# A fused two-block transformer kernel: scan operations in another order, squares of the norms added on GpSimd, rotary halves swapped by DMA

## The chip, the cores and the metric

The kernel runs on one core of a Trainium2 chip. A core has TensorE (PE in the profile; PEld is its weight load), VectorE (DVE), ScalarE (ACT), GpSimd (POOL) and the sync engine (SP), each with its own instruction stream; they wait for one another through semaphores. All numbers are float32. The metric is the time of one execution on the device in microseconds (us); lower is better.

## The reference, cut to what matters

256 tokens go through a first block (attention in three branches, a gated feed-forward part with a short convolution), and then, beside 256 context tokens, through two layers of a second block. The width is 1024. What the change touches:

```python
def rmsnorm(x, g, eps=1e-6):
    xf = x.astype(jnp.float32)
    y = xf * lax.rsqrt(jnp.mean(xf * xf, axis=-1, keepdims=True) + eps)
    return (y * g.astype(jnp.float32)).astype(x.dtype)

def apply_rope(x, cos, sin):            # on q and k of the latent tokens
    ...
    return jnp.concatenate([x1 * c - x2 * s, x1 * s + x2 * c], axis=-1).astype(x.dtype)

def ssd_chunked(x, dt, a, bm, cm, h0, need_y):   # once forward, once backward
    ...
    cb = jnp.einsum('bclgn,bcsgn->bclsg', cc, bc)
    y = (jnp.einsum('bclsg,bclsgr,bcsgrp->bclgrp', cb, lmat, xc)
         + jnp.einsum('bclgn,bcgrpn,bclgr->bclgrp', cc, h_in, jnp.exp(cs)))

def ssd_output(yf, yb, xs, z, ssd_d, ssd_norm_g, w_ssd_o):
    y = (yf + yb + ssd_d[:, None] * xs).reshape(b, n, SSD_D_INNER)
    return rmsnorm(y * jax.nn.silu(z), ssd_norm_g) @ w_ssd_o

def merge(att, ssd, ga, gs):
    return (jax.nn.sigmoid(ga) * (att @ w_attn_o) + jax.nn.sigmoid(gs) * ssd) @ w_out
```

`x` of the scan is the output of a convolution over 5 tokens (its taps) and a silu.

## The kernel before

Activations lie in SBUF with the features on the 128 partitions: `X` is the residual stream, `H` the normed input, 8 tiles of 512 columns (columns 0 to 255 are the latent tokens, 256 to 511 the context). All weights come as one stream of 1 MB chunks (128 x 8 x 256) through a ring of four buffers, loaded by SP as soon as TensorE is done with the chunk four before. A chunk of 16 matmuls writes two PSUM banks of a pair in `PB`; two pairs take turns, and TensorE waits on `evacuated` until VectorE and ScalarE have read a pair. The order on every engine is written out by hand, and each step waits for counts of semaphores. Layer 0 of the second block works on T = 512 columns (latent and context), layer 1 mostly on 256. `pe_fast` is a variant of a projection with seven products for eight, for which GpSimd first makes four sums of each weight chunk (`pool_sums`, L498 to L503, two chunks ahead), and VectorE puts the results together (`dve_fast`).

**Norms.** The squares of a norm's 8 tiles are written to SBUF, and `norm_sums` (L582) has TensorE add them over partitions and tiles: 8 matmuls with a matrix of 1/1024. ScalarE takes the root (`norm_root`, L589), VectorE the reciprocal (L595), then multiplies each tile (L2060), ScalarE adds the shift (L1499). For n2, n4, m21 and final (`sums_behind`) the matmuls of tiles 0 and 1 follow the second group of the projection before, those of 2 and 3 the third, those of 4 to 7 the last. m10c is the norm of the context columns, behind the first group of `down`. For m20 and m11 (512 columns) all eight stand at the end: VectorE adds the last result to `X` (L2376), ScalarE squares it (L599), TensorE sums.

**Rotary part.** While TensorE computes the four chunks of v (L1043), it also multiplies each of the 16 tiles of q and k by a matrix `rot` that swaps halves of 32 rows with a sign (L1066), one after each fourth of a chunk. VectorE multiplies the result by sin (L2100), GpSimd the tile by cos (L2485), VectorE adds (L2105). A barrier of all engines follows.

**Scan.** `scan_group` runs for 8 groups. Per group TensorE transposes (L1177), makes chunk states (L1198), applies them (L1212) and computes the products inside a chunk (`within`, L1229; 4 a group in layer 0, 2 in layer 1), and between these it projects the next group (L1146) and z (L1127). VectorE updates states and reads their results (`states`, L2233 to L2250), adds the skip product D*x (L2253), multiplies the decays with the scores (`masked`, L2265), applies the taps of the next group (`taps`, L2202; this frees the banks), and adds the inner products to Y (`sum_y`, L2272). At the end stand four chunks of gates gs (`project_gs`, L1160), the sum of squares of the normed output (L1282), its root (L1723) and the sigmoids of the gates (L1728).

The loop in VectorE's order:

```python
for g in range(SSD_GROUPS):
    states(g)
    per = 4 // len(units)
    for u in range(len(units)):
        masked(g, u)
        taps(g + 1, range(per * u, per * u + per))
    sum_y(g)
```

## Time and profile before

| | us |
|---|---|
| median of 3 runs | 3190.84 (3190.33 to 3196.2) |
| the profiled execution | 3196.1 |
| its span, first to last instruction | 3194.3 |
| TensorE busy | 3053.8 (96%) |
| VectorE busy | 1194.8 (37%) |
| ScalarE busy | 779.6 (24%) |
| GpSimd busy | 522.9 (16%) |
| mean granted TensorE clock | 0.987 |

Times in the rows are from the span's start. A row of a timeline is a group of equal instructions: start, length to the end of the last, engine, line, operation, output and inputs, count, and in square brackets the idle time of the engine ahead of it and what ended it. A float matmul has two records, so x16 are eight matmuls. The length of a row of matmuls includes the drain of the last; the difference of two starts does not. The granted clock is 1.00 for 2.4 GHz; its lower level is 1.2 GHz.

### The profile page before, as it was taken

Reading aid. Unit: us, or ns where it says so; the run is one execution under the profiler, and the core shown is the slowest. Engines: PE = TensorE matmul, PEld = TensorE weight load, DVE = VectorE, ACT = ScalarE, POOL = GpSimd, SP = SyncE. Lnnn points to the kernel's source line nnn. Section 1 sums busy time; section 2 is a strip of 40 time slices with the busy share of each in tenths; the row PEclk is TensorE's granted clock in tenths of the full one; section 3 lists DMA queues with packets and bytes.
Section 4 is the critical chain, followed back from the end, with each engine's and each line's share of the span. In section 5 each row is a group of like instructions: output and inputs, shape, how many; then the busy total and the mean of one; then the engine's idle time right before and its main releaser. Section 6 shows DMA issues by size and latency. Waiting matters only on the chain.

```text
span 3194.3 us, 35650 instructions
## 1 busy us (share of the span) xinstructions
PE 3053.8 (96%) x13958; PEld 2288.5 (72%) x13958; DVE 1194.8 (37%) x2286; ACT 779.6 (24%) x1697; POOL 522.9 (16%) x544
## 2 busy tenths in 40 slices
PE   8989899999999999999999999999999999989998
PEld 6766788887865545555548688887876766678887
DVE  1244232213236645555533542333146555531100
ACT  1012121201013324555520120111013355530000
POOL 0000110002210101121234233442210011110100
PEclk9999999999999999999999999999999999999999
DMA  6455334442235222222212122222211332224342
GB/s 232 155 210 203 119 120 156 149 143 90 93 115 215 93 94 92 106 93 98 88 60 86 66 93 79 93 87 85 93 66 53 120 106 93 105 97 153 132 158 93
DMA packets 60830, 365.66 MB, mean 114 GB/s; under 512 B 5818, under 2 KB 17146, under 8 KB 18320
## 3 DMA queue, kind: packets, MB, share of 16 engines
q1 hardware_dynamic: 48768, 334.67, 29.2%
q10 hardware_dynamic: 10944, 25.36, 2.3%
q0 software_dynamic: 976, 3.63, 0.3%
q8 instruction: 101, 1.65, 0.2%
q14 instruction: 41, 0.34, 0.0%
HBM read 362.37 MB, written 1.28 MB: 114 GB/s over the span
## 4 chain that ended last, share of the span: by engine, by line
PE 88%; DVE 8%; ACT 2%; issue 2%; DMA 0%; POOL 0%; POOLq 0%; DVEq 0%; ACTq 0%
PE PB L348 11%; PE PB L1146 10%; PE PB L465 9%; PE PB L392 9%; PE PB L974 7%; PE PA L465 6%; PE PB L1127 6%; PE PB L867 6%; PE PS L465 5%; PE PB L1043 3%; PE PB L1160 3%; DVE work L2202 2%; PE PA L1229 1%; PE PA L1198 1%; PE PA L1212 1%
## 5 line engine op out<-in xcount | busy, mean ns | idle before, releaser
L1146 PE MATMUL PB<-H,ring 128*128 128x512 f32 (+1 forms) x1024 | 428.1, 566 | 0.0
L1146 PEld LDWEIGHTS PB<-H,ring 128*128 128x128 f32 x1024 | 191.8, 190 | 184.6 <-issue 179.1
L392 PE MATMUL PB<-work,ring 128*128 128x256 f32 x1280 | 277.6, 379 | 0.0
L392 PEld LDWEIGHTS PB<-work,ring 128*128 128x128 f32 x1280 | 243.2, 190 | 33.1
L348 PE MATMUL PB<-H,ring 128*128 128x256 f32 x960 | 213.0, 385 | 10.4 <-ACT H L1499 7.5
L974 PE MATMUL PB<-H,ring 128*128 128x256 f32 x992 | 214.3, 379 | 0.0
L348 PEld LDWEIGHTS PB<-H,ring 128*128 128x128 f32 x960 | 185.4, 193 | 38.0 <-issue 12.0
L974 PEld LDWEIGHTS PB<-H,ring 128*128 128x128 f32 x992 | 188.5, 190 | 25.6
L1127 PE MATMUL PB<-H,ring 128*128 128x512 f32 (+1 forms) x512 | 182.0, 508 | 14.9 <-DVE work L2202 14.9
L2202 DVE SCALAR_TENSOR_TENSOR work<-PB,par,work 128x510 f32<-128x510 f32 (+3 forms) x256 | 181.0, 713 | 12.6 <-ACT work L1594 5.8
L867 PE MATMUL PB<-H,ring 128*128 128x256 f32 (+1 forms) x640 | 179.7, 436 | 1.5 <-ACT mod L1387 0.9
L348 PE MATMUL PB<-work,ring 128*128 128x256 f32 (+1 forms) x544 | 155.8, 446 | 7.1 <-POOL work L2446 2.4
L867 PEld LDWEIGHTS PB<-H,ring 128*128 128x128 f32 x640 | 122.6, 197 | 49.5 <-issue 35.3
L1127 PEld LDWEIGHTS PB<-H,ring 128*128 128x128 f32 x512 | 98.9, 199 | 78.5 <-issue 70.5
L465 PE MATMUL PB<-work,sums 128*128 128x256 f32 x680 | 150.8, 379 | 0.0
L2519 POOL TENSOR_TENSOR work<-work 128x256 f32<-128x256 f32 x96 | 59.7, 643 | 542.6 <-ACT work L1616 440.6
L498 POOL TENSOR_TENSOR sums<-ring 128x512 f32<-128x512 f32 x53 | 69.0, 1301 | 469.7 <-PE PA L465 224.3
L348 PEld LDWEIGHTS PB<-work,ring 128*128 128x128 f32 x544 | 104.1, 192 | 56.5 <-issue 37.8
L465 PEld LDWEIGHTS PB<-work,sums 128*128 128x128 f32 x680 | 129.2, 190 | 17.6
L1655 ACT ACTIVATE work<-sums,work 128x128 f32<-128x128 f32 x384 | 117.1, 389 | 81.8 <-PE PA L1229 81.4
L465 PE MATMUL PA<-work,sums 128*128 128x256 f32 x528 | 118.5, 379 | 0.0
L1043 PE MATMUL PB<-ring,H 128*128 128x256 f32 x512 | 115.7, 379 | 0.0
(326 smaller groups left out, 4344.6 us busy)
## 6 DMA issues: line engine op xcount, KB each, us to landing
ring<-stream SPq DMA_DIRECT2D x315, 1024.0 KB, 4.8
sums<-cs_rows ACTq DMA_DIRECT2D x16, 1024.0 KB, 4.8
sums<-cs_rows ACTq DMA_DIRECT2D x16, 512.0 KB, 3.9
work<-scratch POOLq DMA_DIRECT2D x1, 2560.0 KB, 14.1
X<-xT SPq DMA_DIRECT2D x2, 1024.0 KB, 16.0
out<-H SPq DMA_DIRECT2D x1, 1024.0 KB, 4.8
con<-consts SPq DMA_DIRECT2D x1, 716.0 KB, 17.9
wdt<-w_dt POOLq DMA_DIRECT2D x1, 512.0 KB, 10.5
```

The source lines that it names most:

```text
L348: mm = pe.matmul(PB[:, pair, t, 0:T], ring[:, c % SLOTS, k, t * P:(t + 1) * P], rhs(k), start=(k == 0), stop=(k == KT - 1))
L392: mm = pe.matmul(PB[:, pair, t, 0:T], ring[:, c % SLOTS, k, t * P:(t + 1) * P], rhs(KT * part + k), start=(part == 0 and k == 0), stop=(pa ...
L465: mm = pe.matmul(fast_bank(side, bank)[:, col:col + T1], weight(k), right(4 * part + k), start=first and opens and k == 0, stop=last and k ...
L498: nc.gpsimd.tensor_tensor(su[:, 0], a21, a22, ALU.add).then_inc(sem("w_summed"), 1)
L867: mm = pe.matmul(PB[:, pair, t, 0:T], ring[:, c % SLOTS, k, t * P:(t + 1) * P], H[:, k, 0:T], start=(k == 0), stop=(k == KT - 1))
L974: mm = pe.matmul(PB[:, pair, t, 0:T1], ring[:, c % SLOTS, k, t * P:(t + 1) * P], h1(k), start=(k == 0), stop=(k == KT - 1))
L1043: mm = pe.matmul(PB[:, pair, t // 2, CHUNK * (t % 2):CHUNK * (t % 2 + 1)], H[:, k, t * P:(t + 1) * P], ring[:, c % SLOTS, k, :], start=(k ...
L1127: mm = pe.matmul(PB[:, pair, t, 0:T], ring[:, c % SLOTS, k, t * P:(t + 1) * P], H[:, k, 0:T], start=(k == 0), stop=(k == KT - 1))
L1146: mm = pe.matmul(PB[:, pair, t, 0:Tc], ring[:, c % SLOTS, k, t * P:(t + 1) * P], H[:, k, 0:Tc], start=(k == 0), stop=(k == KT - 1))
L1160: mm = pe.matmul(PB[:, pair, t, 0:T], ring[:, c % SLOTS, k, t * P:(t + 1) * P], H[:, k, 0:T], start=(k == 0), stop=(k == KT - 1))
L1655: ins = copy(MB[n % 2][:, r, d, t, :], BC[:, q, r, d, (t0 + t) * P:(t0 + t + 1) * P], ACT.Relu, scale=-1.0, bias=CS[:, t0 + t, hh:hh + 1])
L2202: ins = vec.scalar_tensor_tensor(dst, src, par[:, W0 + 32 * tap + ch:W0 + 32 * tap + ch + 1], dst, ALU.mult, ALU.add)
```

## The change

It has four parts.

1. Norms n2, m10c, n4, m20, m11, m21 and final: GpSimd adds the squares of tiles 2 and 3, then 4 and 5, onto those of 0 and 1 (for m10c also 6 and 7) and then tile 1 onto tile 0 (`add_squares`). TensorE sums tiles 0, 6 and 7 at the end (`norm_added`), for m10c tile 0 alone, and that behind the second group of `down`.
2. The 32 rotation matmuls go. ScalarE's queue issues four DMAs of 32 partitions for q and four for k, which write the swapped halves to `ROT_T`; the sign is in the table of sines. VectorE and GpSimd multiply and add four tiles at a time, and VectorE copies one chunk of v after each of these four steps.
3. In the scan, `masked(g, 0)` moves ahead of the last state reads, in layer 1 with the taps of the next group's first tile before it; the skip product moves to the head of `sum_y`.
4. Three gate chunks stand ahead of the sum of squares, where two stood (one of the four is spread through the last group), and ScalarE opens chunk 0 ahead of the last `gain`, chunk 1 ahead of the root.

```diff
+        def norm_added(pe, tag, T, sq):
+            pe.wait_ge(sem("squares_added"), ADDED.index(tag) + 1)
+            tiles = (0,) if tag == "m10c" else (0, 6, 7)
+            for k in tiles:
+                if k:
+                    squared(pe, tag, k + 1)
+                mm = pe.matmul(sums_to(tag)[:, 0:T], full(ONE_D), sq(k), start=(k == 0), stop=(k == tiles[-1]))
+            mm.then_inc(sem("norm_sum"), 1)
+
+        def add_squares(pool, tag, sq):
+            steps = [(0, 2, 4), (0, 4, 6)] + ([(0, 6, 8)] if tag == "m10c" else [])
+            for to, at, n in steps:
+                squared(pool, tag, n)
+                nc.gpsimd.tensor_tensor(sq(to, 2), sq(to, 2), sq(at, 2), ALU.add).then_inc(sem("squares_pairs"), 1)
+                pairs_added[0] += 1
+                pool.wait_ge(sem("squares_pairs"), pairs_added[0])
+            nc.gpsimd.tensor_tensor(sq(0, 1), sq(0, 1), sq(1, 1), ALU.add).then_inc(sem("squares_added"), 1)
...
                 def after(j):
-                    for i in (j - 1, j) if j == 3 else (j - 1,) if j else ():
-                        norm_sums(pe, tag, T1, lambda k: SQ[:, k, 0:T1], (2 * i, 2 * i + 1), 2 * i)
-                    if j == 0 and tag == "n4":
-                        norm_sums(pe, "m10c", T1, lambda k: SQ[:, k, T1:TT], range(KT))
+                    if j == 3:
+                        norm_added(pe, tag, T1, lambda k: SQ[:, k, 0:T1])
+                    if j == 1 and tag == "n4":
+                        norm_added(pe, "m10c", T1, lambda k: SQ[:, k, T1:TT])
...
-                for n in range(4):
-                    project_gs(1, n // 2, n % 2)
+                for n in range(8):
+                    project_gs(1 + n // 4, n // 2 % 2, n % 2)
                 pe.wait_ge(sem("s_y"), LAYER["s_y"] * (la + 1))
                 pe.wait_ge(sem("s_sum"), LAYER["s_sum"] * (la + 1))
                 pe.matmul(PA[0][:, 0:T], full(ONE), SQ_SUM[:, 0:T], start=True, stop=True).then_inc(sem("z_sum"), 1)
-                for n in range(8):
-                    project_gs(2 + n // 4, n // 2 % 2, n % 2)
+                for n in range(4):
+                    project_gs(3, n // 2, n % 2)
...
+                def swap_halves(n, tiles):
+                    for to in range(4):
+                        act.dma_start(ROT_T[32 * to:32 * to + 32, KT * n:KT * n + KT, :],
+                                      tiles[32 * (to ^ 1):32 * (to ^ 1) + 32, :, 0:T1]).then_inc(swapped[n], 16)
+
+                swap_halves(0, LQ)
                 act_fast(act, f"k{la}", Q_KEEP)
+                fast_done(act, f"k{la}")
+                swap_halves(1, LK)
...
+                act.wait_ge(sem("s_within"), LAYER["s_within"] * la + len(units) * SSD_GROUPS)
+                gates(0)
+                gain(SSD_GROUPS - 1)
+                gates(1)
+                act.wait_ge(sem("s_y"), LAYER["s_y"] * (la + 1))
+                act.wait_ge(sem("z_sum"), la + 1)
+                copy(RSTD[:, 0:T], PA[0][:, 0:T], ACT.Sqrt, scale=1.0 / SSD_INNER, bias=EPS_C).then_inc(sem("z_root"), 1)
+                gates(2)
+                gates(3)
...
+                        if i == 2:
+                            if la:
+                                taps(g + 1, (0,))
+                            masked(g, 0)
                         for d, order in enumerate((F_ORDER, B_ORDER)):
...
-                        masked(g, u)
-                        taps(g + 1, range(per * u, per * u + per))
+                        if u:
+                            masked(g, u)
+                        taps(g + 1, range(max(la, per * u), per * u + per))
```

`LAYER["rot_sin"]` and `LAYER["rot_cos"]` become 4, and `const_parts` loses `rot`. In GpSimd's program `add_squares("m20", ...)` stands between the weight sums of `out20` and those of `mlp1a0`, and `add_squares("m11", ...)` behind those of `mlp2b0`.

VectorE in a group of the second layer's scan, before: L2235 is the last state update, L2249 and L2250 the reads, L2253 the skip product, L2265 the mask, L2202 the taps of tiles 0 and 1.

```order
L2235 TENSOR_TENSOR work<-work,PA 128x256
L2249 TENSOR_TENSOR work<-PA,work 128x256
L2250 TENSOR_TENSOR work<-work 128x2x128
L2249 TENSOR_TENSOR work<-PA,work 128x256
L2250 TENSOR_TENSOR work<-work 128x2x128
L2253 SCALAR_TENSOR_TENSOR work<-work,par 128x256 x2
L2265 TENSOR_TENSOR work<-work 128x1024
L2202 SCALAR_TENSOR_TENSOR work<-PB,par,work 128x2x254
```

The same place in the changed kernel, whose lines are L2263 (state update), L2230 (taps), L2292 (mask), L2281 and L2282 (reads):

```order
L2263 TENSOR_TENSOR work<-work,PA 128x256
L2230 SCALAR_TENSOR_TENSOR work<-PB,par,work 128x2x254
L2230 SCALAR_TENSOR_TENSOR work<-PB,par,work 128x2x255 x2
L2230 SCALAR_TENSOR_TENSOR work<-PB,par,work 128x2x254
L2292 TENSOR_TENSOR work<-work 128x1024
L2281 TENSOR_TENSOR work<-PA,work 128x256
L2282 TENSOR_TENSOR work<-work 128x2x128
L2281 TENSOR_TENSOR work<-PA,work 128x256
L2282 TENSOR_TENSOR work<-work 128x2x128
```

Four taps and the mask multiply moved ahead of the two pairs of reads; the skip product is no longer there.

GpSimd at m20 in the changed kernel: L505 ends the weight sums of `out20`'s last chunk, L605 and L608 are the additions of squares, and the sums of `mlp1a0`'s first chunk start with L500.

```order
L505 TENSOR_TENSOR sums<-ring,sums 128x512
L605 TENSOR_TENSOR work<-work 128x1024 x2
L608 TENSOR_TENSOR work<-work 128x512
L500 TENSOR_TENSOR sums<-ring 128x512
L501 TENSOR_TENSOR sums<-ring 128x512
```

The weight sums of the next two chunks, which followed one another before, now stand behind additions that wait for tile 5's square.

ScalarE at the end of the second layer's scan, before: L1667 and L1670 are the last `gain`, L1723 the root, L1728 the sigmoids of all four chunks.

```order
L1679 ACTIVATE work<-PB 128x256 x2
L1667 ACTIVATE work<-work,par 128x256 x2
L1670 ACTIVATE work<-work 128x2x256
L1723 ACT_TABLE_LOAD
L1723 ACTIVATE rstd<-PA,small 128x256
L1728 ACT_TABLE_LOAD
L1728 ACTIVATE work<-PB 128x256 x8
```

In the changed kernel L1701 is the silu of z, L1747 the sigmoids, L1689 and L1692 the `gain`, L1755 the root:

```order
L1701 ACTIVATE work<-PB 128x256 x2
L1747 ACT_TABLE_LOAD
L1747 ACTIVATE work<-PB 128x256 x2
L1689 ACTIVATE work<-work,par 128x256 x2
L1692 ACTIVATE work<-work 128x2x256
L1747 ACTIVATE work<-PB 128x256 x2
L1755 ACT_TABLE_LOAD
L1755 ACTIVATE rstd<-PA,small 128x256
L1747 ACT_TABLE_LOAD
L1747 ACTIVATE work<-PB 128x256 x4
```

Half of the sigmoids moved ahead of the root, with one table load more.

## Rows read from the trace of the kernel before

**Rows 1.** The page: busy time of the engines, and the chain that ended last.

```profile
PE 3053.8 (96%) x13958; PEld 2288.5 (72%) x13958; DVE 1194.8 (37%) x2286; ACT 779.6 (24%) x1697; POOL 522.9 (16%) x544
...
PE 88%; DVE 8%; ACT 2%; issue 2%; DMA 0%; POOL 0%; POOLq 0%; DVEq 0%; ACTq 0%
```

**Rows 2.** Waits of TensorE: total us, times, longest us.

```profile
PE PB L1127 <- DVE work L2202: 14.9, 7, 2.1
...
PE PB L1160 <- ACT work L1728: 8.6, 2, 4.6
```

**Rows 3.** Timeline of TensorE at n2 and m10c: start us, us, what.

```profile
378.81 1.03 PE L582 MATMUL PA<-work,small 128*128 128x256 f32 x4
...
395.75 1.13 PE L582 MATMUL PA<-work,small 128*128 128x256 f32 x4 [0.37 <-DVE work L1992]
...
656.71 3.62 PE L582 MATMUL PA<-work,small 128*128 128x256 f32 x16
```

**Rows 4.** Timeline of TensorE at m20 (two rows) and m11.

```profile
1810.15 5.31 PE L582 MATMUL PB<-work,small 128*128 128x512 f32 x12
1817.38 1.98 PE L582 MATMUL PB<-work,small 128*128 128x512 f32 x4 [1.92 <-ACT work L599]
...
2213.20 7.44 PE L582 MATMUL PB<-work,small 128*128 128x512 f32 x16
```

**Rows 5.** Timeline of VectorE at m10, m20 (two rows) and m11.

```profile
763.10 5.22 DVE L2060 SCALAR_TENSOR_TENSOR H<-X,mod,rstd 128x256 f32<-128x256 f32 x8
...
1813.21 3.45 DVE L2376 SCALAR_TENSOR_TENSOR X<-work,mod,X 128x256 f32<-128x256 f32 x4
...
1821.76 3.26 DVE L2060 SCALAR_TENSOR_TENSOR H<-X,mod,rstd 128x256 f32<-128x256 f32 x8
...
2216.26 1.67 DVE L2376 SCALAR_TENSOR_TENSOR X<-work,mod,X 128x256 f32<-128x256 f32 x4
```

**Rows 6.** Timeline of GpSimd at m20: the last weight sum there.

```profile
1814.26 1.33 POOL L503 TENSOR_TENSOR sums<-ring,sums 128x512 f32<-128x512 f32 x1
```

**Rows 7.** Timeline of TensorE in the v stage and behind it, layer 0.

```profile
862.16 0.59 PE L1066 MATMUL PS<-work,con 128*128 128x256 f32 x2
862.59 3.62 PE L1043 MATMUL PB<-ring,H 128*128 128x256 f32 x16
...
922.46 1.13 PE L1079 MATMUL PS<-work 64*128 64x512 f32 x4 [1.42 <-DVEq L284]
```

**Rows 8.** Timeline of VectorE: the copy of the last chunk of v.

```profile
920.64 0.69 DVE L2111 COPY work<-PB 128x512 f32<-128x512 f32 x1 [2.15 <-PE PB L1043]
```

**Rows 9.** The page: ScalarE's DMA queue (packets, MB, share), its 1 MB loads.

```profile
q10 hardware_dynamic: 10944, 25.36, 2.3%
...
sums<-cs_rows ACTq DMA_DIRECT2D x16, 1024.0 KB, 4.8
```

**Rows 10.** Timeline of TensorE: the first inner product of a group, layer 0.

```profile
1324.85 1.09 PE L1229 MATMUL PA<-work 128*64 128x128 f32 x16 [1.09 <-issue]
```

**Rows 11.** Timeline of VectorE: the mask multiply ahead of it.

```profile
1323.52 1.22 DVE L2265 TENSOR_TENSOR work<-work 128x1024 f32<-128x1024 f32 x1
```

**Rows 12.** Timeline of TensorE: z behind the first inner product, two groups, layer 1.

```profile
2589.68 3.69 PE L1127 MATMUL PB<-H,ring 128*128 128x256 f32 x16 [2.14 <-DVE work L2202]
...
2631.39 5.38 PE L1127 MATMUL PB<-H,ring 128*128 128x256 f32 x16 [2.13 <-DVE work L2202]
```

**Rows 13.** Timeline of VectorE: the taps of tiles 0 and 1.

```profile
2583.44 6.09 DVE L2202 SCALAR_TENSOR_TENSOR work<-PB,par,work 128x508 f32<-128x508 f32 x8
```

**Rows 14.** Stretches: length, TensorE busy (records), granted clock, DMA share, GB/s.

```profile
1620.00:1640.00 20.00, 15.39 (x30) 0.83 0.14 53
2630.00:2640.00 10.00, 8.61 (x43) 0.83 0.23 97
```

**Rows 15.** Timeline of TensorE: the last two gate chunks, layer 0 and layer 1.

```profile
1629.47 30.72 PE L1160 MATMUL PB<-H,ring 128*128 128x512 f32 x64 [4.61 <-ACT work L1728]
...
2849.50 15.74 PE L1160 MATMUL PB<-H,ring 128*128 128x256 f32 x64 [3.96 <-ACT work L1728]
```

More of the change, by code:

```diff
@@ L271, in program @@
         }
+        ADDED = ["n2", "m10c", "n4", "m20", "m11", "m21", "final"]
         SUMMED = ["n1", "n2", "n3", "m10c", "n4", "m10", "m20", "m11", "m21", "final"]
@@ L1719, in _, with gates @@
                     silu_z(g)
[L1720 to L1724 removed]
+                def gates(j):
                     pair, _ = GROUPS[f"gs{la}"][j]
@@ L2552, in _ @@
                 repeat(pool, n // 4, square)
+                add_squares(pool, "final", lambda k, n: SQ[:, k:k + n, 0:T1])
 def _weights(w):
```

105 lines of the change are left out of this document (45 added, 60 removed).

## The prediction

> **What bounds the kernel now.** I read the page first: TensorE is busy 3053.8 of 3194.3 us, and the chain that ended last is 88% TensorE [rows 1]. So two things can shorten the run: matmuls that are no longer issued while TensorE has nothing else to wait for, and the 140.5 us in which it stands still. The waits of TensorE, sorted, say who holds it [rows 2]: 14.9 us in seven waits for VectorE's taps (L2202), and 8.6 us in two waits for ScalarE's sigmoids (L1728); each scan group of the first layer adds 1.09 us before L1229 [rows 10]. The change touches all three. Last I read the timelines of each place that it edits, and the granted clock there. A float matmul is two records in them; 256 columns take 0.43 us (16 records of L1043 take 3.45 us from start to start), 512 columns 0.88 us.
>
> **The change part by part.** The sum is made against the span of 3194.3 us and then taken from the median, 3190.84; the profiled execution took 3196.1, which the runs reach too (3196.2), so the gain is carried over as a difference.
>
> *Norm matmuls.* Seven norms have their squares added on GpSimd: six need 3 matmuls for 8, the context norm m10c 1 for 8. What matters is where the missing ones stood. In n2, n4, m21 and final, tiles 0 to 3 were summed between chunks, 4 records in 0.86 us after each of two chunks, in a stretch with no wait; that is 1.7 us each. Tiles 4 and 5 at the tail lay beside the evacuation of the last chunk (0.37 us was still waited [rows 3]), so they give nothing. 4 x 1.7 = 6.9. m10c: 8 matmuls stood between two chunks, the 16 records of 656.71 [rows 3]; 7 x 0.43 = 3.0. The additions for these five are hidden: two of 128x512 and one of 128x256, 1.3 + 1.3 us and half of that by the nearest row [rows 6], the last started when tiles 4 and 5 are squared, a whole chunk (6.9 us or 27.6 us) before they are needed. Together **9.9 us**.
>
> *m20 and m11* are different: all eight matmuls stand at the end, while VectorE adds the last tiles to X and ScalarE squares them. In m20 TensorE did six, waited 1.92 us for the last two; in m11 it did eight in 7.44 us without a wait [rows 4]. So five fewer are worth about nothing, and the additions now compete. VectorE's last four updates of X took 3.45 us with GpSimd adding beside them for most of that time and 1.67 us with it idle; the eight multiplies by 1/rms took 5.22 us with GpSimd busy for the first half, 3.26 without [rows 5]. So each us of GpSimd beside such work costs VectorE about 0.75 us (1.96 over 2.6). In m20 the 128x1024 addition (2.5 us) starts when tile 5 is squared, 1811.8, the 128x512 one ends near 1816, and behind them in GpSimd's order stand the eight sums for mlp1a0's first two chunks, 10.4 us that were done before 1815.6 until now. The updates of X go from 3.45 to about 5.9 (+2.4), and the multiplies, with GpSimd busy for 3 us more, lose 2.1: **-4.5 us**. In m11 nothing follows: 2.4 us of additions beside the updates, +1.8; and TensorE now stands idle from 2213.2 for 5.6 us until the sum is there, where it worked until 2220.5. Behind such waits the rows show the lower clock (below); I take one such loss, 1.7: **-3.5 us**. Bounds for both places: 0 (what the change leaves if GpSimd costs nothing), and -14 (VectorE's eight multiplies wait one addition of 1.3 us each, +7 in m20, and one more low-clock stretch and the full addition in each).
>
> The Trainium skill (SBUF — State Buffer, Who interferes with whom) says that a VectorE instruction with two SBUF inputs and a GpSimd instruction that reads SBUF exclude each other for a whole instruction. The row of 3.45 us bears that out. Taken literally, the first update of X waits for the rest of the 128x1024 addition, and the two places come to -4.4 and -4; the sum moves by less than 1 us.
>
> *Rotary.* 32 matmuls (64 records of L1066) go, each between v chunks that follow without a wait: 862.16 to 862.59 is 0.43 us [rows 7]. 32 x 0.43 = 13.8. After the last v chunk came one more rotation, its multiply and its addition, then the barrier: the next matmul started at 922.46, 2.0 us after the chunk's end. Now the copy of v ends the stage, 0.69 us [rows 8] plus the 0.2 us ahead of it and 0.1 behind; with the last rotation's own 0.43 taken off, 1.6 becomes 1.0, rounded down to 0.5 us more in each layer [rows 7]. **14.8 us.** What it adds: 8 DMAs a layer on ScalarE's queue, 0.4 us each to issue beside ScalarE's idle time (nothing is queued behind them but k's and v's copies, 12 us apart); 1 MB each for q and k. The nearest row is 4.8 us to land for 1 MB on that queue [rows 9]. q is swapped from about 815 and needed after 862; k is swapped from about 862, and TensorE would only feel it if it came after the last v chunk at 914. Four GpSimd multiplies of 128x1024 (2.5 us) and eight VectorE operations (1.2 us) lie in the same 50 us. Price 0; the cover is 45 us in each layer. VectorE now waits for a DMA ahead of the copies of v that free TensorE's banks: the third v chunk needs the first copy, at 886, only after q's swap.
>
> *Scan, first layer.* In each of eight groups TensorE waited 1.09 us before its first product with the mask: VectorE's mask multiply ended at 1324.74, and TensorE started at 1324.85 [rows 10, 11]. That multiply stood behind the two reads and the skip product (1.41 us). Now it runs at 1318.2, before TensorE has the reads ready, in idle time of VectorE; the skip product moves behind the taps, where VectorE waits for TensorE anyway. 8 x 1.09 = **8.7 us**.
>
> *Scan, second layer.* Seven waits of 2.13 us for the second tile's taps, which end at 2589.5 [rows 12, 13]. Now tile 0's taps (3.05) and the mask (1.22) go in front of the reads. By the same durations: taps 0 to 2580.1, mask to 2581.3, reads to 2583.0 (1.7 later than before, but TensorE asks for them at 2586.4), taps 1 to 2586.1, and TensorE asks for the bank at 2587.5. The wait goes, with 1.4 us to spare; next late would be the second mask, ready 4 us before it is asked for. 14.9, and 0.5 in the last group. In four of the seven groups the 16 records after the wait took 5.38 us and not 3.69 [rows 12]: the granted clock of 2630 to 2640 is 0.83 [rows 14], so a part of it ran at 1.2 GHz and not 2.4. Where TensorE only waited 1.09 us (first layer) no group shows that. With the waits gone I take all four back, 6.8; the bound is 0. **22.2 us.**
>
> *Gates.* After the first two gate chunks TensorE waited 4.61 us in the first layer and 3.96 in the second for ScalarE's sigmoids of chunk 0, which stood behind the root and two table loads [rows 15]. Now chunk 0's sigmoids run right after the last product, the pair is free 10 us early, and the sum of squares is one chunk later, with the fourth chunk (13.8 and 6.9 us) covering root and tables (about 5). The waits go. The rows after them took 30.72 and 15.74 us where the same records at full clock take 27.7 and 14.0; the granted clock of 1620 to 1640 is 0.83 [rows 14]. 4.6 + 2.9 + 4.0 + 1.7 = **13.2 us**.
>
> Sum: 9.9 + 14.8 + 8.7 + 22.2 + 13.2 - 4.5 - 3.5 = 60.8 us. 3190.84 - 60.8 = **3130 us**.
>
> **The rivals.** (a) *The clock is not given back.* TensorE stays at 1.2 GHz for as long as before, at other places (behind m20 and m11, and at the starts of attention), where waits stay or grow (the 1.92 us at m20 [rows 4] is one). For it: three of the seven waits of 2.13 us were followed by no low clock, so a wait is not enough, and what decides is not in the rows. Against it: all six stretches priced here follow waits that go. It takes back 6.8 + 2.9 + 1.7 = 11.4: 3141. (b) *GpSimd costs the full bound* at m20 and m11: 14 instead of 8, 3136; with (a) 3147. (c) *VectorE becomes the bound of the second scan*: reads and taps trade places only, and the wait moves from the bank to the reads, 1.7 us in each of seven groups, with the four clock losses kept: 11.9 + 6.8 taken back, 3149. Against it is the slack of 3.4 us at the reads. (d) *GpSimd costs nothing*: 3122. (e) *Slower than before*: the swap between partitions. Its rows are 1 KB long, 1024 a swap, and no row of the trace moves such pieces inside the chip. If all ran one after the other on one engine at some 0.11 us (2.3% of 16 engines' span over 10944 packets [rows 9]), k's swap would land 110 us after 862, 58 us after the last v chunk, in both layers: +116 - 61, 3246. It decides from 82 us of landing on, where the two layers lose 60 together; below 50 us nothing shows.
>
> The Trainium skill (DMA: Bandwidth & Descriptors, Why a DMA increments its semaphore by 16 and not by 1) lets the outermost dimension choose the engines, 16 for these 32 partitions. By that rule (e) is out; no row here shows it.
>
> **How the numbers follow.** The forecast 3130, with 4 us either way, has 0.50; (d) 0.12; (b) 0.10; (a) 0.13; (a) with (b), and (c), 0.10 together; (e) 0.03; 0.02 for a small change of either sign. From 3116 (GpSimd free and some clock given back at attention) to 3150 holds all but some 0.1 of this. A measurement of this kernel can tell about 0.2% (6 us) from no change. Faster by more than that: 0.95. Within: 0.02. Slower: 0.03.
>
> **What would show it.** TensorE's waits lose the rows of L2202, L1229 and the sigmoids; its records fall by 138 (74 of norms, 64 of rotations); the span of v's four chunks is 55.3 us and the next matmul 1 us later. At m20 and m11 VectorE's four updates of X take over 3.4 us and TensorE waits longer than before. Granted clock above 0.987 speaks for the 11.4 us; equal to it, for (a). Wrong would be: a wait of TensorE in the v stage (DMA), a wait for the reads in the second scan, or an unchanged wait at the gates.

## The result, and the profile after

The changed kernel took 3137.26 us in the median of four executions (3131.18, 3131.31, 3143.22 and 3143.51), the kernel before 3192.06 (3190.33 to 3196.2): 0.983 of the time, 95% interval 0.981 to 0.984, 54.8 us less. The forecast was 3130 us, 60.8 less, with 3116 to 3150 as its range. Two executions came within 1.3 us of it, two were 12 us slower; one of these slower ones was profiled (3143.51, span 3141.7, mean granted clock 0.984; its neighbour had 0.983, the two at 3131 us 0.988).

The page of the changed kernel, engines and chain, answers to [rows 1]:

```profile
PE 3024.4 (96%) x13820; PEld 2267.1 (72%) x13820; DVE 1194.7 (38%) x2238; ACT 782.2 (25%) x1699; POOL 556.2 (18%) x542
...
PE 92%; DVE 5%; ACT 2%; issue 1%; DMA 0%; POOL 0%; DVEq 0%; ACTq 0%; POOLq 0%
```

TensorE has 138 records fewer, as forecast, and is on 92% of the chain for 88%. Its waits, longest sum first, answer to [rows 2]:

```profile
PE PB L596 <- POOL work L608: 11.0, 2, 5.5
...
PE PB L349 <- ACT H L1505: 7.5, 2, 3.9
```

The rows for the taps, the products with the mask and the sigmoids are gone. A new one leads: two waits of 5.5 us of `norm_added` for GpSimd's additions, at m20 and m11.

**Where the time went.** I put the rows of TensorE's two timelines side by side and read by how much each starts earlier than before. A part's gain is the difference between two such leads, which no other part enters.

| part | read at start (before / after) | lead before it, behind it | measured | forecast |
|---|---|---|---|---|
| n2 | 402.05 / 400.16 | 0, 1.9 | 1.9 | 1.7 |
| m10c, n4 | 747.13 / 740.50 | 1.9, 6.6 | 4.7 | 4.7 |
| 1.2 GHz behind m10 | 774.10 / 768.98 | 6.6, 5.1 | -1.5 | 0 |
| rotary, layer 0 | 922.46 / 909.84 | 5.1, 12.6 | 7.5 | 7.4 |
| end of attention, layer 0 | 1186.08 / 1180.15 | 12.6, 5.9 | -6.7 | 0 |
| scan, layer 0 | 1595.02 / 1579.82 | 5.9, 15.2 | 9.3 | 8.7 |
| gates, layer 0 | 1661.53 / 1638.46 | 15.2, 23.1 | 7.9 | 7.5 |
| m20 | 1838.51 / 1820.65 | 23.1, 17.9 | -5.2 | -4.5 |
| m11 | 2252.59 / 2240.96 | 17.9, 11.6 | -6.2 | -3.5 |
| rotary, layer 1 | 2364.78 / 2345.66 | 11.6, 19.1 | 7.5 | 7.4 |
| attention, layer 1 | 2377.70 / 2357.30 | 19.1, 20.4 | 1.3 | 0 |
| scan, layer 1 | 2832.23 / 2789.25 | 20.4, 43.0 | 22.6 | 22.2 |
| gates, layer 1 | 2865.08 / 2816.20 | 43.0, 48.9 | 5.9 | 5.7 |
| m21, final | 3194.3 / 3141.7 (spans) | 48.9, 52.6 | 3.7 | 3.4 |

The rows behind it, in the changed kernel's timelines: TensorE's four chunks of v and the next matmul [rows 7], a first inner product of layer 0 [rows 10], z behind the first inner product of a group of layer 1 [rows 12], and the last gate chunks [rows 15].

```profile
853.59 55.42 PE L1069 MATMUL PB<-ring,H 128*128 128x256 f32 x256
909.84 1.13 PE L1085 MATMUL PS<-work 64*128 64x512 f32 x4 [0.83 <-DVEq L285]
...
1315.44 1.09 PE L1235 MATMUL PA<-work 128*64 128x128 f32 x16
...
1623.24 13.90 PE L1166 MATMUL PB<-H,ring 128*128 128x512 f32 x32
...
2563.21 3.72 PE L1133 MATMUL PB<-H,ring 128*128 128x256 f32 x16
...
2809.30 7.07 PE L1166 MATMUL PB<-H,ring 128*128 128x256 f32 x32
```

Except at the barrier behind v, none of these rows has an idle time in brackets, and none is stretched: 3.72 us where [rows 12] has 5.38 in four groups of seven.

**m20.** TensorE from out20's last row to mlp10n, before and after; [rows 4] has what stands between before.

```profile
1808.42 1.89 PE L465 MATMUL PA<-work,sums 128*128 128x256 f32 x8
...
1822.93 9.26 PE L1006 MATMUL PB<-H,ring 128*128 128x256 f32 x34 [3.58 <-ACT H L1499]
```

```profile
1785.36 1.89 PE L467 MATMUL PA<-work,sums 128*128 128x256 f32 x8
1792.73 2.05 PE L596 MATMUL PB<-work,small 128*128 128x512 f32 x2 [5.49 <-POOL work L608]
1796.39 3.37 PE L596 MATMUL PB<-work,small 128*128 128x512 f32 x4 [1.61 <-ACT work L625]
1804.12 2.47 PE L1032 MATMUL PB<-H,ring 128*128 128x256 f32 x5 [4.35 <-ACT H L1505]
```

14.51 us became 18.76. VectorE and GpSimd in the changed kernel, in the same stretch and (the last row) at m11, against [rows 5]:

```profile
1790.15 5.53 DVE L2409 SCALAR_TENSOR_TENSOR X<-work,mod,X 128x256 f32<-128x256 f32 x4
...
1802.17 4.04 DVE L2089 SCALAR_TENSOR_TENSOR H<-X,mod,rstd 128x256 f32<-128x256 f32 x8
...
1788.85 2.34 POOL L605 TENSOR_TENSOR work<-work 128x1024 f32<-128x1024 f32 x1 [9.80 <-ACT work L625]
1791.27 1.32 POOL L608 TENSOR_TENSOR work<-work 128x512 f32<-128x512 f32 x1
...
2198.40 3.52 DVE L2409 SCALAR_TENSOR_TENSOR X<-work,mod,X 128x256 f32<-128x256 f32 x4
```

The updates of X went from 3.45 to 5.53 us, those at m11 from 1.67 to 3.52. The last four records of the sum took 3.37 us for 1.98: they ran at 1.2 GHz.

**The end of layer 0's attention.** Two stretches of the changed kernel, and the same two of the kernel before (columns: length, TensorE's busy time, its weight loads, VectorE, ScalarE, GpSimd, granted clock, DMA share, GB/s):

```profile
1060.00:1080.00 20.00, 16.71 (x90) 14.47 (x89) 8.57 (x25) 11.30 (x23) 2.04 (x2) 0.72 0.16 53
1080.00:1100.00 20.00, 20.00 (x56) 11.74 (x56) 13.60 (x14) 5.46 (x7) 3.21 (x3) 0.77 0.00 0
```

```profile
1060.00:1080.00 20.00, 17.57 (x66) 9.03 (x65) 7.97 (x22) 5.09 (x21) 0.00 (x0) 1.00 0.15 53
1080.00:1100.00 20.00, 19.14 (x102) 13.32 (x103) 10.25 (x19) 11.79 (x12) 4.24 (x4) 1.00 0.00 1
```

A granted clock of 0.72 and 0.77 over 40 us means about 20 us at 1.2 GHz. The 64 records for dt show the cost:

```profile
1071.49 13.91 PE L1256 MATMUL PS<-wdt,H 128*128 128x64 f32 x64 [0.40 <-ACTq L285]
```

They took 7.36 us before. From the last products of attention to the second projection of the scan 9.3 us were lost; 2.6 of them came back behind it, where TensorE had stood idle before the change (1.80 us for VectorE and some smaller gaps). That is the 6.7 of the table.

### The profile page after: what moved, and what is told of

Read it like the earlier page. It is cut to its first block, busy times and chain, and to the rows that moved or that the text cites. A ratio compares the mean times of both kernels' runs of the same rounds, so it can differ in the third digit from the quotient of the medians.

```text
span 3141.7 us, 35319 instructions
## 1 busy us (share of the span) xinstructions
PE 3024.4 (96%) x13820; PEld 2267.1 (72%) x13820; DVE 1194.7 (38%) x2238; ACT 782.2 (25%) x1699; POOL 556.2 (18%) x542
## 4 chain that ended last, share of the span: by engine, by line
PE 92%; DVE 5%; ACT 2%; issue 1%; DMA 0%; POOL 0%; DVEq 0%; ACTq 0%; POOLq 0%
PE PB L1152 13%; PE PB L349 11%; PE PB L467 10%; PE PB L393 9%; PE PB L1000 7%; PE PA L467 6%; PE PB L893 6%; PE PB L1133 5%; PE PS L467 5%; PE PB L1069 4%; PE PB L1166 3%; PE PA L1235 2%; PE PA L1204 1%; PE PA L1218 1%; PE PB L371 1%; ACT work L1574 1%
## 5 line engine op out<-in xcount | busy, mean ns | idle before, releaser
L2230 DVE SCALAR_TENSOR_TENSOR work<-PB,par,work 128x510 f32<-128x510 f32 (+3 forms) x256 | 181.6, 713 | 24.1 <-ACT work L1616 17.3
L500 POOL TENSOR_TENSOR sums<-ring 128x512 f32<-128x512 f32 x53 | 69.3, 1307 | 426.0 <-PE PA L467 213.5
L2066 DVE SCALAR_TENSOR_TENSOR work<-PB,par,work 128x254 f32<-128x254 f32 (+1 forms) x128 | 55.8, 477 | 159.2 <-ACT work L1491 155.0
## 6 DMA issues: line engine op xcount, KB each, us to landing
work<-scratch POOLq DMA_DIRECT2D x1, 2560.0 KB, 13.8
```

The source lines that it names most:

```text
L500: nc.gpsimd.tensor_tensor(su[:, 0], a21, a22, ALU.add).then_inc(sem("w_summed"), 1)
L2230: ins = vec.scalar_tensor_tensor(dst, src, par[:, W0 + 32 * tap + ch:W0 + 32 * tap + ch + 1], dst, ALU.mult, ALU.add)
```

## The experiments

Twelve runs were made; the first is the changed kernel again. A comparison of two profiles has a trap: executions start differently. By n2 the nine profiles of the changed kernel and of what was made from it, whose code is the same up to there, lie up to 5.7 us apart (394.59 in c1_sums_later, 397.12 in a1_after, 400.33 in c3_best), and the granted clock of the first matmuls differs, here in the changed kernel and in a2_sums_back:

```profile
20.00:40.00 20.00, 18.36 (x71) 15.64 (x72) 5.08 (x11) 0.77 (x2) 0.63 (x1) 0.83 0.81 275
```

```profile
20.00:40.00 20.00, 19.18 (x89) 16.95 (x90) 4.26 (x11) 0.77 (x2) 1.20 (x1) 1.00 0.90 324
```

So what a kernel did at a place is read from steps between leads, as above. The total is given by medians, and these carry the difference at the start too: where one is set against a theory that lies a few us off, the profiles' time from n2 to the end stands beside it. From n2 on the steps repeat: from out20's last row to mlp10n it is 18.8 us, from there to mlp1a0 16.5, and from q1 to k1 31.4, within 0.1 us in the profiles of the changed kernel, a1_after, a4_layer1_back and b4_norms. (Where a kernel has the norms' part, the 1.9 us of n2 itself are counted in.)

| kernel | median us (executions) | kernel before, same chip | ratio, 95% interval |
|---|---|---|---|
| a1_after | 3140.57 (3138.55 to 3141.06) | 3192.47 | 0.984 (0.982 to 0.985) |
| a2_sums_back | 3132.80 (3124.11 to 3134.02) | 3192.47 | 0.981 (0.980 to 0.982) |
| a3_unread | 3137.00 (3129.28 to 3139.59) | 3192.47 | 0.983 (0.982 to 0.984) |
| a4_layer1_back | 3163.00 (3161.77 to 3166.85) | 3192.47 | 0.991 (0.989 to 0.992) |
| b1_scan | 3160.75 (3159.81 to 3161.89) | 3190.83 | 0.991 (0.989 to 0.992) |
| b2_gates | 3182.60 (3180.14 to 3184.68) | 3190.83 | 0.997 (0.996 to 0.998) |
| b3_rotary | 3179.50 (3178.10 to 3182.38) | 3190.83 | 0.996 (0.995 to 0.998) |
| b4_norms | 3194.42 (3186.86 to 3197.43) | 3190.83 | 1.001 (1.000 to 1.002) |
| c1_sums_later | 3139.37 (3125.29 to 3139.66) | 3189.91 | 0.983 (0.981 to 0.985) |
| c2_busy_wait | 3137.40 (3128.28 to 3139.39) | 3189.91 | 0.982 (0.981 to 0.984) |
| c3_best | 3130.52 (3123.48 to 3135.45) | 3189.91 | 0.980 (0.979 to 0.982) |
| d1_busy_behind | 3123.84 (3115.06 to 3126.53) | 3192.82 | 0.977 (0.976 to 0.979) |

**The changed kernel again.**

> The changed kernel once more, unedited. Its four executions lay at 3131.2 and 3131.3, and at 3143.2 and 3143.5 us. In the profile of one of the latter, TensorE has 1.2 GHz from the last products of layer 0's attention to the start of its scan (23.7 us from start to start for what took 14.5 before, 9.3 more). Theory: this one stretch makes the two groups, so the times fall into the same two groups again, some 12 us apart, with the mean granted clock 0.988 in one and 0.984 in the other. Rival: the groups belong to the chip or the hour; then all of them lie in one group here, or somewhere between.

All five lie within 2.5 us, at 3138.6 to 3141.1, with a granted clock of 0.985, and the profiled one has the low stretch at the same place. So one group of times here, not two: the theory's groups didn't come back. Nor does the stretch alone make 12 us. One kernel made from the changed one, a3_unread, was profiled without it, at 3129.3 (clock 0.989), where its other four executions took 3136.7 to 3139.6 (0.986):

```profile
1060.00:1080.00 20.00, 17.94 (x103) 13.09 (x104) 10.17 (x23) 12.97 (x17) 4.23 (x4) 1.00 0.00 1
1080.00:1100.00 20.00, 20.00 (x48) 8.93 (x47) 19.83 (x11) 4.08 (x6) 4.16 (x4) 1.00 0.15 53
```

The code up to there is the same as in the changed kernel. From n2 to the start of the scan a3_unread took 772.2 us and the changed kernel 780.0: 6.0 less behind attention, and 1.8 less ahead of it, most of it behind m10. Add up to 5.7 for the start, and executions of one program can lie up to 13.5 us apart; the two pairs of the result were 12. That is an estimate from profiles of several kernels: none of the executions at 3131 was profiled. The other kernels fit it: except for a3_unread's, every profile of the changed kernel and of what was made from it has the stretch, and each kernel's fastest execution lies below its profiled one, at 3129.9 in a2_sums_back (five executions from 3124.1 to 3134.0), 3136.3 in c1_sums_later (3125.3 to 3139.7) and 3123.9 in d1_busy_behind (3115.1 to 3126.5). None of the profiles of the kernel before and of b1 to b4 shows it.

**The additions of m20 and m11 taken out.**

```diff
-        ADDED = ["n2", "m10c", "n4", "m20", "m11", "m21", "final"]
+        ADDED = ["n2", "m10c", "n4", "m21", "final"]
...
-                    norm_added(pe, "m20", TT, lambda k: SQ_OUT[:, k, :])
+                    norm_sums(pe, "m20", TT, lambda k: SQ_OUT[:, k, :], range(KT))
...
-                    add_squares(pool, "m20", lambda k, n: SQ_OUT[:, k:k + n, :])
```

(and the same for m11)

> The changed kernel with the additions of m20 and m11 taken out: TensorE sums all eight tiles of these two again. By the traces the two places cost 4.25 + 0.95 us (m20) and 3.23 + 3.0 us (m11), the second number of each being matmuls behind them at 1.2 GHz. Theory: all of it comes back, 11.4 us below the run of the changed kernel with the same clock at the end of attention, so about 3120 (3132 with the low stretch there); from the last chunk of out20 to mlp10n 12.8 us, from the last chunk of mlp2b0 to q1 11.0. Rival (the clock is lost at other places whatever TensorE waits for): 7.5 us minus 3.9 kept, 3127.

7.8 us below a1_after. In the trace m20 gives 4.3 + 1.2 us, m11 3.2 + 1.3 (6.2 was expected), and 1.6 are lost again, most of it behind m21; from n2 to the end it is 8.3 us. The steps at the two places are back to those of before, 12.8 and 11.0 us. Of the low clock only a part is: behind m11 1.7 us stay, and a stretch behind m21 got longer. 10.0 of the theory's 11.4 us came at the two places; the total is nearer to the rival's 7.5: the slower VectorE and the waits go entirely, the clock does not.

**The same additions, read by nobody.**

```diff
+        UNREAD = {"m20": area(22528, 2, TT), "m11": area(23808, 2, TT)}
...
+            for k in range(KT):
+                squared(pe, tag, k + 1)
+                if k == KT - 1:
+                    pe.wait_ge(sem("squares_added"), ADDED.index(tag) + 1)
+                mm = pe.matmul(sums_to(tag)[:, 0:T], full(ONE_D), sq(k), start=(k == 0), stop=(k == KT - 1))
```

> GpSimd makes the same additions for m20 and m11 at the same place in its program, but into an area that nothing reads; TensorE sums all eight tiles, as soon as each is squared, and looks at the end of the additions only ahead of the eighth, long after it. What the output needs is computed as before the change. It parts the cost of 11.4 us in two. Theory (GpSimd's work slows VectorE's beside it; TensorE's wait for the sum costs through the clock alone): the updates of X stay at 5.5 and 3.5 us and the first multiplies of m20 at 4.0 (4.7 us of cost stay), while the 1.2 GHz at the sums and behind goes, 6.7 us: 3124.5. Rival 1 (the chain through GpSimd's additions is what costs): all 11.4 go, updates of X at 3.4 and 1.7, 3120. Rival 2 (the low clock comes with the slower VectorE or at a place of its own, whatever TensorE does): nothing goes, 3131.

VectorE and TensorE at m20, VectorE at m11, and the granted clock of the two places:

```profile
1778.19 5.54 DVE L2430 SCALAR_TENSOR_TENSOR X<-work,mod,X 128x256 f32<-128x256 f32 x4
...
1784.45 3.06 PE L606 MATMUL PB<-work,small 128*128 128x512 f32 x4 [4.01 <-ACT work L646]
...
2185.42 3.53 DVE L2430 SCALAR_TENSOR_TENSOR X<-work,mod,X 128x256 f32<-128x256 f32 x4
...
1780.00:1800.00 20.00, 11.33 (x35) 7.49 (x34) 15.54 (x23) 9.87 (x21) 11.04 (x9) 0.74 0.01 2
2190.00:2210.00 20.00, 16.43 (x66) 13.19 (x65) 15.26 (x27) 7.96 (x20) 1.04 (x1) 0.91 0.14 52
```

5.54 and 3.53 us stay, though nobody waits for the sums. Rival 1 falls: GpSimd's work beside VectorE costs even where the sums don't go through GpSimd. The step from out20 to mlp10n is still 18.76 us, as in the changed kernel. The clock came back at m11 (1.4 + 1.5 us by the steps), and behind m20 for 1.0 us. In m20 itself TensorE did six of eight sums early but then waited 4.0 us for VectorE's slow updates, and the last two sums ran slower behind that wait as well (3.06 us for 1.98). In all 3.9 us come back by the steps, and 3.6 below a1_after by the medians, where the theory had 6.7; the two kernels' intervals overlap, so it is the steps that carry this.

**Layer 1's scan in its old order.**

```diff
-                        if i == 2:
-                            if la:
-                                taps(g + 1, (0,))
+                        if i == 2 and not la:
                             masked(g, 0)
```

(and mask, taps and skip product of layer 1 where they stood)

> The changed kernel with VectorE's order in the second layer's scan as it was: reads, skip product, mask, taps of tiles 0 and 1. Layer 0 keeps the new order. Theory: the seven waits of 2.1 us for the taps come back (14.9, and 0.5 in the last group), and with them four stretches at 1.2 GHz, one in every second group or so (6.8): 22 us above the changed kernel, 3153, and the mean granted clock some 0.002 lower. Rival (the clock does not hang on these waits): 15.4 us above, 3146.5, with the granted clock of the scan at 1.00 throughout.

22.4 us above a1_after, and 22.6 at the end of this scan in the trace. Waits of TensorE, and one group:

```profile
PE PB L1133 <- DVE work L2230: 14.9, 7, 2.1
...
2569.35 5.38 PE L1133 MATMUL PB<-H,ring 128*128 128x256 f32 x16 [2.13 <-DVE work L2230]
...
2612.75 3.69 PE L1133 MATMUL PB<-H,ring 128*128 128x256 f32 x16 [2.14 <-DVE work L2230]
```

Seven waits of 2.1 us, and again 5.38 us in four groups and 3.69 in three. Four of the seven waits bring the 1.2 GHz with them, as before the change, though the kernel reaches them some 20 us earlier, and without the waits none of it is there. The rival's 15.4 us falls. Which of the waits do it is still not in the rows: before, it was the first, third, fifth and seventh, here the first, second, fifth and seventh.

**The parts alone.** Each adds one part of the change to the kernel before, with the code of the diff shown ahead.

> The kernel before with the scan's new order on VectorE alone (mask ahead of the last reads, in layer 1 the first taps ahead of it, skip product in the sum). Theory: the parts of the change are independent, and this one gives what the forecast has for it, 8.7 in layer 0 and 22.2 in layer 1, of which 6.8 are matmuls no longer at 1.2 GHz: 30.9 us below the kernel before, with no stretch of the second scan under 1.00 of granted clock. Rival (the low clock in the second scan hangs on the weight on TensorE over a longer time, and was lifted by other parts of the change): 24 us.

30.1 us below the kernel before (31.3 from n2 to the end in the profiles), as the theory has it; the rival's 24 falls. In the trace 9.3 in layer 0 and 22.8 in layer 1, and the second scan ran at full clock:

```profile
2540.00:2795.00 255.00, 252.49 (x1109) 166.04 (x1109) 145.04 (x267) 142.01 (x297) 52.70 (x83) 1.00 0.31 107
```

> The kernel before with the gates' part alone (three chunks ahead of the sum of squares, ScalarE opens chunk 0 ahead of the last gain). Theory: 4.6 + 2.9 + 4.0 + 1.7 = 13.2 us below the kernel before, TensorE's waits for the sigmoids gone. Rival (the clock stays low behind other waits): 8.6 us.

8.2 us by the medians (5.4 to 11.5 by the interval), 11.0 from n2 to the end in the profiles: less than the theory's 13.2, and the rival's 8.6 can't be told from it. At the gates themselves the trace has 7.9 + 5.9 us, what the theory says and a little more, low clock included. But, in the rival's way, at m20 and m11, which this kernel leaves alone, 1.7 and 1.6 us more are spent than before, and the granted clock is lower there than it was (0.91 around m20, 1.00 around m11):

```profile
1800.00:1820.00 20.00, 14.51 (x38) 8.15 (x37) 14.91 (x27) 9.43 (x21) 4.39 (x4) 0.83 0.13 52
2200.00:2220.00 20.00, 16.29 (x51) 10.42 (x50) 12.88 (x28) 7.78 (x18) 0.00 (x0) 0.91 0.14 53
```

> The kernel before with the rotary part alone (swap by DMA, no rotation matmuls). Theory: 7.5 us in each layer as in the whole change, 15 in all; span of the four chunks of v 55.3 us. Rival (part of the gain in the whole change came from the other parts): under 12 us.

11.3 us by the medians, with an interval from 7 to 16 that holds the theory's 15 and the rival's 12, and 13.0 from n2 to the end in the profiles. At the two places it is 7.5 each, as expected, but 4.3 us more than before are spent from m20 to behind m11 (steps of 0.9, 0.7 and 2.8), where nothing was edited; 2.3 of them are won back elsewhere.

> The kernel before with the norms' part alone (squares of all seven norms added on GpSimd). Theory: n2, m10c, n4, m21 and final give 10.3 us, m20 and m11 take 7.5 by slower updates of X and TensorE's wait, and 4 more by matmuls at 1.2 GHz: within 2 us of the kernel before. Rival (the clock is lost there only in the whole change, where TensorE is busier): 3 us below it.

3.6 us above, with an interval that reaches from nothing to 0.2% slower, and 1.1 above from n2 to the end in the profiles: no gain, as the theory has it; the rival's 3 us of gain isn't there. At m20 and m11 the steps are those of the whole change (4.2 + 1.0 and 3.3 + 3.0). So seven norms of additions are worth nothing, five of them about 10 us.

The four medians add up to 46.0 us; the whole change gave 51.9 in a1_after's executions. The profiles from n2 to the end have 31.3 + 11.0 + 13.0 - 1.1 = 54.2 us for the parts and 52.6 for the whole. So the parts add up within 2 us, though only the whole has the low stretch behind attention.

**GpSimd's weight sums moved away from VectorE's updates.**

```diff
+                    pool.wait_ge(sem("norm_rstd"), ROOTED.index("m20b") + 1)
                     for name in ("mlp1a0", "mlp2a0", "mlp1b0", "mlp2b0"):
                         pool_sums(pool, name)
```

> The changed kernel without the additions of m20 and m11 (TensorE sums eight tiles there), and with GpSimd's weight sums for mlp1a0 held back at m20 until VectorE has the second reciprocal. It takes GpSimd's work away from beside VectorE's updates of X, in a place where it always stood: there they took 3.45 us before the change, and 1.67 at m11, where GpSimd was idle. Theory (VectorE pays for what GpSimd does beside it): the four updates take 1.7 us, the step from out20's last chunk to mlp10n 11.0 us instead of 12.8, the multiplies of the second half some 0.8 longer; in all 1 to 2 us below a2_sums_back. Rival (the updates of m20 are slow for a reason of their own, two operations of ScalarE or the DMA beside them): 3.4 us stay, and the weight sums come later for nothing, 0 to +2.

VectorE's updates and its second eight multiplies by 1/rms, and GpSimd beside them:

```profile
1784.59 1.67 DVE L2409 SCALAR_TENSOR_TENSOR X<-work,mod,X 128x256 f32<-128x256 f32 x4
...
1796.31 11.44 DVE L2089 SCALAR_TENSOR_TENSOR H<-X,mod,rstd 128x256 f32<-128x256 f32 x8
...
1797.58 1.46 POOL L501 TENSOR_TENSOR sums<-ring 128x512 f32<-128x512 f32 x1
```

The same multiplies one by one, min/median/max in ns, in this kernel and in the kernel before:

```profile
L2089 DVE SCALAR_TENSOR_TENSOR H<-X,mod,rstd x8: 1479/1485/1590, 1796.3 to 1806.3; 128x256 f32<-128x256 f32 x8
```

```profile
L2060 DVE SCALAR_TENSOR_TENSOR H<-X,mod,rstd x16: 479/480/486, 1821.8 to 1829.5; 128x256 f32<-128x256 f32 x16
```

The updates fell to 1.67 us, and out20 to mlp10n by 1.8 us, as the theory says. But the eight multiplies of the second half took 11.44 us for 3.26. The theory had 0.8 us for them; it was 8. In all the kernel is 6.6 us above a2_sums_back by the medians, and 6.7 from n2 to the end in the profiles, where 1 to 2 below was expected. Each waits until GpSimd's running instruction (1.3 to 1.5 us) ends, then runs, then GpSimd's next begins: eight multiplies beside eight sums, one for one. The Trainium skill (SBUF — State Buffer, Who interferes with whom) says that a VectorE instruction with two SBUF inputs and a GpSimd one that reads SBUF exclude each other; this trace agrees, and its number for it is 1.0 us more per instruction of 0.48. Here that is 0.74 us per us of GpSimd (8.2 over 11.1), so the prediction's rule of 0.75 holds as an average; what failed is how much of GpSimd's work was taken to lie beside VectorE's. What counts is how many VectorE instructions meet how many of GpSimd's. By counting, [rows 5] follow too: two of the four updates of 3.45 us waited for one sum each, and in the changed kernel's 5.53 us all four did (1.32 to 1.48 us each).

**TensorE kept busy ahead of the additions.**

```diff
+            for k in range(n):
+                pe.matmul(bank[:, 0:T], full(ONE_D), src[:, k, 0:T], start=True, stop=True)
...
+                    busy(pe, "m20", 5)
                     norm_added(pe, "m20", TT, lambda k: SQ_OUT[:, k, :])
```

> The changed kernel with five matmuls of 128x512 whose results nobody reads in front of TensorE's wait for GpSimd's additions, at m20 and at m11. The wait was 5.5 us, five matmuls take 4.3. Nothing on the path moves; only TensorE stands still for less. Theory (the 1.2 GHz at these two places, 1.4 + 0.95 and 1.4 + 3.0 us, comes from TensorE's idle time): the sums of tiles 0, 6 and 7 and the chunks behind run at 2.4 GHz, 5 to 6.7 us below the changed kernel. Rival (it comes from what was computed long before, or at its own times): no gain, 0.

TensorE at m20 and at m11, and the clock around each:

```profile
1787.83 1.12 PE L596 MATMUL PB<-work,small 128*128 128x512 f32 x2 [1.11 <-POOL work L616]
1791.58 3.45 PE L596 MATMUL PB<-work,small 128*128 128x512 f32 x4 [2.62 <-ACT work L633]
...
2197.89 1.98 PE L596 MATMUL PB<-work,small 128*128 128x512 f32 x4 [0.61 <-ACT work L633]
...
1780.00:1800.00 20.00, 11.99 (x30) 5.80 (x29) 12.21 (x16) 6.05 (x12) 14.07 (x10) 0.86 0.16 53
2190.00:2210.00 20.00, 14.70 (x43) 8.66 (x42) 15.92 (x30) 8.96 (x21) 3.68 (x2) 0.91 0.15 52
```

At m11 the last four records run at 2.4 GHz again (1.98 us) and 2.7 us come back, 1.4 to q1 and 1.3 behind it. At m20, where waits of 1.1, 2.6 and 4.3 us were left, nothing does. By the medians no difference to the changed kernel can be told. Of the 5 to 6.7 us of the theory 2.7 came: right at one place, not at the other.

**TensorE kept busy behind the sums**, first on top of c1_sums_later (four such matmuls behind m20 and m11, eight of 256 columns behind m21), then on top of a2_sums_back, with two more between tiles 5 and 6 of m20:

```diff
-                    norm_sums(pe, "m20", TT, lambda k: SQ_OUT[:, k, :], range(KT))
+                    norm_sums(pe, "m20", TT, lambda k: SQ_OUT[:, k, :], range(6))
+                    busy(pe, "m20", 2)
+                    norm_sums(pe, "m20", TT, lambda k: SQ_OUT[:, k, :], (6, 7), 6)
+                    busy(pe, "m20", 4)
```

> c1_sums_later with such idle matmuls behind the sums of m20 and m11 (four of 128x512 each) and of m21 (eight of 128x256), where TensorE waits 3.6 to 3.9 us for the normed tiles. Theory: the low clock behind these three waits goes, 1.7 + 1.7 us and up to 3.4 at m21: 4 to 7 us below c1_sums_later. Rival (waits of that length don't bring it): 0, or above, if the idle matmuls end after the tiles are ready (0.1 us each place).

8.9 us below c1_sums_later by the medians, with intervals that just overlap; by the steps 1.7 at m20, 2.9 at m11, 3.0 at m21, and 6.6 from n2 to the end in the profiles, in the theory's range.

> The changed kernel without the additions of m20 and m11 (TensorE sums eight tiles, GpSimd's weight sums stand where they always did), and with matmuls whose results nobody reads in TensorE's waits: at m20 two of 128x512 ahead of tile 6 (1.9 us of wait) and four behind the sums (3.6), at m11 four, at m21 eight of 128x256 (3.9). Theory (idle time of TensorE brings the 1.2 GHz behind it, and this is all that such matmuls change): against a2_sums_back the low clock behind m20 and m11 goes (1.2 + 1.3 us by the step from mlp10n to mlp1a0 and from q1 to k1) and that at m21 (3.4 us at most): 3 to 6 us below its 3132.8 us, so 3127 to 3130. What c3_best showed speaks for it: there the steps behind m11 and m21 fell by 2.9 and 3.0. Rival (the low stretches return elsewhere later): no gain at the end. The stretch of 20 us at the end of layer 0's attention, which divides the executions in two, is not touched.

The granted clock around m20, m11 and m21, first in a2_sums_back, then here:

```profile
1780.00:1800.00 20.00, 14.52 (x44) 8.97 (x43) 13.99 (x24) 9.01 (x19) 5.05 (x4) 0.91 0.14 54
...
2180.00:2200.00 20.00, 16.29 (x52) 10.46 (x51) 11.83 (x25) 6.72 (x16) 0.00 (x0) 0.92 0.15 52
...
2880.00:2900.00 20.00, 15.11 (x55) 12.18 (x54) 5.88 (x11) 5.78 (x12) 0.91 (x2) 0.83 0.21 81
```

```profile
1780.00:1800.00 20.00, 19.65 (x63) 11.45 (x62) 13.87 (x24) 8.87 (x19) 5.06 (x4) 1.00 0.15 54
...
2180.00:2200.00 20.00, 19.72 (x67) 12.27 (x66) 13.11 (x28) 8.00 (x19) 0.00 (x0) 1.00 0.15 52
...
2880.00:2900.00 20.00, 18.57 (x85) 15.78 (x84) 6.31 (x12) 6.16 (x13) 1.04 (x1) 1.00 0.29 106
```

All three are at 1.00. The steps are 1.4, 1.7 and 3.1 us, the profiled execution is 6.0 us shorter, and the low stretches did not return later: the rival falls. This is the fastest kernel of the study, 69.0 us below the kernel before. Eighteen matmuls that compute nothing made it faster than the same kernel without them: its ratio to the kernel before, 0.977 (0.976 to 0.979), does not overlap with that of a2_sums_back, 0.981 (0.980 to 0.982), nor with that of the changed kernel in a1_after, 0.984 (0.982 to 0.985).

## Why the prediction was right, and where it was not

*Norm matmuls*: right, 10.3 us for 9.9. The additions of n2, m10c, n4, m21 and final are hidden; b4_norms shows the whole part to be worth nothing once m20 and m11 are in it.

*Rotary*: right, 15.0 for 14.8, and 7.5 in each layer in b3_rotary too. Rival (e) was out by far. The page has the swaps, and the timelines ScalarE's issues for k and the GpSimd multiply that waits for them:

```profile
work<-work ACTq DMA_DIRECT2D x16, 256.0 KB, 4.4
...
856.71 3.64 ACTq L1551 DMA_DIRECT2D work<-work  x4
...
864.23 4.67 POOL L2521 TENSOR_TENSOR work<-work,con 128x1024 f32<-128x1024 f32 x2 [24.81 <-DMA work<-work]
```

4.4 us to land each, k usable 7.5 us after the first issue, with 45 us of cover.

*Scan, layer 0*: 9.3 for 8.7; 1.16 a group, since the start-to-start difference is what counts and not the idle time of 1.09. *Scan, layer 1*: 22.6 for 22.2, with the four losses of clock taken back; a4_layer1_back shows them to hang on the waits. Rival (c) fell. *Gates*: 13.8 for 13.2.

*m20 and m11*: the sum was -8.0, measured -11.4. The updates of X were right (+2.1 and +1.9 for +2.4 and +1.8). The multiplies at m20 lost 0.8 and not 2.1: GpSimd ended at 1803.15, and one of the eight met it. That -5.2 at m20 came near -4.5 is therefore luck, since too much for the multiplies stood against too little for the clock. The clock term was mis-sized: 0 taken at m20, where 1.4 us went in the sum and 1.0 behind it; 1.7 at m11, where it was 1.4 and 3.0. Rival (b), whose bound was 14, lay a little nearer to it than the forecast's 8. Its reason for 7 of the 14, eight multiplies that wait one GpSimd instruction each, did not happen here; it is what c1_sums_later then showed, with 8.2.

*What no step priced*: 1.5 us behind m10 and 6.7 net at the end of layer 0's attention. The prediction looked at the places it edits and at the waits there; this one is no edit. Together these two are 8.2 us, just what the profile's 52.6 lacks of the forecast's 60.8. The other misses cancelled, which is luck: m20 and m11 lost 3.4 us more than forecast, and all the rest together gained some 3.4 more. The two executions at 3131.2, with a granted clock of 0.988, fit the absence of that stretch and a quick start; but no profile of them exists, so their nearness to 3130 is no proof of the sum.

*Rival (a)* had 0.13 and the words "the clock is not given back". The truth lies between: at each place priced it was (scan and gates at 1.00), and part of it was lost elsewhere, as b2_gates and b3_rotary show with 3 to 4 us each at m20 and m11, of which 0.5 and 2.3 came back at other unedited places. "Granted clock above 0.987 speaks for the 11.4 us" was a bad sign to name: it was 0.984 and 0.988, while the 11.4 us were all won at their places. A mean over the run can't tell a gain here from a loss there.

**Still open**: what makes the first 400 us of some executions up to 5.7 us longer; what brings the 20 us of 1.2 GHz at the end of layer 0's attention in some executions, when the same instructions in the same order run at 2.4 GHz in others; and which waits of 2.1 us are followed by the low clock.

## What to carry to other kernels

A reduction taken from TensorE pays where TensorE had nothing to wait for, and costs where another engine's chain ends last: ask of each place which engine that is, and leave the places of the second kind alone. Beside a GpSimd instruction, count VectorE's instructions with two SBUF inputs, not its time: each may wait for one whole GpSimd instruction. When waits of TensorE like those at the norms here (1.9 to 3.9 us) can't be removed, matmuls that nobody reads can fill them, if they end before the data come, and should be tried: here 6 us by the traces and 9 by the medians for ten lines. Before two kernels a few us apart are compared, look at where their executions already differ while the code is still the same.

## What the runs showed of the hardware

- VectorE and GpSimd took turns instruction by instruction: 0.48 us became 1.49 for each of eight, while GpSimd's own went from 1.27 to 1.45.
- TensorE was granted 1.2 GHz for about 20 us at the end of layer 0's attention, though busy for 16.7 and 20.0 of the two stretches of 20 us, and only in some executions. It cost 9.3 us where it stood and 6.7 net in the profile of the changed kernel. The clock of the first matmuls differs between executions too (0.83, 0.91 or 1.00 from 20 to 40 us).
- What is faster at one place can bring the low clock at another. With the gates' part alone, m20 and m11 became slower by 3.3 us without an edit there. Filling the waits ended it: 1.00 at all three places.
- The Trainium skill (TensorE: Matmul & The Clock Gate, HAM oscillation — how this bites in real kernels) blames idle gaps of TensorE for the low clock. d1_busy_behind agrees, with 0.91, 0.92 and 0.83 going to 1.00 when the gaps were filled. In the 10 us ahead of the stretch at the end of attention no idle time of TensorE was over 1.2 us; no run here shows what began it.
- A swap of 32-partition blocks by DMA inside SBUF, 256 KB each, landed in 4.4 us.
